# The gated convolution's shifted rows: TensorE products with shift matrices replaced by transfers inside SBUF and VectorE sums

## The reference

```
y_conv = c_b * conv(c_c * c_h, conv_w)        # causal, depthwise, width 3
conv(z)[s] = w[2] * z[s] + w[1] * z[s-1] + w[0] * z[s-2]     # z = 0 ahead of the first token
mix = concat([y_conv, y_gla]) @ w_out
```

## Time and profile before

| | |
|---|---|
| median of three runs | 2489.75 us (2489.63 to 2494.16) |
| profiled execution | 2493.07 us, its span 2491.3 us |
| TensorE matmul busy | 2393.9 us (96%) |
| VectorE busy | 1736.3 us (70%) |
| ScalarE busy | 1300.8 us (52%) |
| GpSimd busy | 100.2 us (4%) |
| DMA | 608.09 MB, mean 244 GB/s |
| mean granted TensorE clock | 0.988 of full |
| end of layer 0's mixer | about 110 to 184 us in the span |
| end of layer 1's mixer | about 455 to 510 us in the span |

### The profile page before, as it was taken

The page is one execution under the profiler, slowest core; times in us unless marked ns, Lnnn a source line. Parts: engine busy times, 40 slices in busy tenths (PEclk is TensorE's granted clock), DMA queues, the critical chain, the costliest instruction groups (busy, mean ns, idle before and its releaser), DMA issues.

```text
span 2491.3 us, 31286 instructions
## 1 busy us (share of the span) xinstructions
PE 2393.9 (96%) x11472; PEld 1927.8 (77%) x11472; DVE 1736.3 (70%) x1986; ACT 1300.8 (52%) x1661; POOL 100.2 (4%) x135
## 2 busy tenths in 40 slices
PE   7999989999999999999998999989999999999997
PEld 3668876768888888888886888878877887897885
DVE  2577775789999999999987446675467443556556
ACT  2334433458877777778873433444344433444442
POOL 1001001000000000000001000000000000000001
PEclk9999999999999999999998999999999999999998
DMA  9869857549999989989986563355536552336550
GB/s 365 302 212 331 321 203 240 182 166 391 393 323 363 393 307 374 380 318 383 362 307 204 175 211 126 118 183 202 202 125 221 181 207 91 125 116 235 202 186 34
DMA packets 316384, 608.09 MB, mean 244 GB/s; under 512 B 15106, under 2 KB 154402, under 8 KB 309603
## 3 DMA queue, kind: packets, MB, share of 16 engines
q1 hardware_dynamic: 306432, 564.27, 63.8%
q0 software_dynamic: 9552, 41.13, 4.5%
q10 hardware_dynamic: 274, 1.05, 0.1%
HBM read 605.31 MB, written 1.08 MB: 243 GB/s over the span
## 4 chain that ended last, share of the span: by engine, by line
PE 85%; DVE 7%; DMA 3%; ACT 2%; issue 1%; POOL 1%; DVEq 0%; ACTq 0%; SPq 0%
PE G L962 49%; PE A L962 29%; PE TB L962 4%; DMA down<-in_ada_w 2%; DVE w_lo L2947 1%; PE TB L1449 1%; POOL small L2755 1%; PE TB L984 1%; PE TB L1558 1%; DMA down<-in_moe_w_down 1%; DVE small L3385 1%; ACT probs L2177 0%; DVE x_tok L3397 0%; DVE u_lo L3291 0%; DVE small L2879 0%
## 5 line engine op out<-in xcount | busy, mean ns | idle before, releaser
L962 PE MATMUL G<-w_hi,u_hi 128*128 128x512 f32 x1592 | 622.2, 397 | 4.5 <-ACT u_hi L2519 2.1
L962 PE MATMUL G<-w_hi,u_lo 128*128 128x512 f32 x1592 | 612.1, 391 | 0.7 <-DVE u_lo L3291 0.7
L962 PE MATMUL G<-w_lo,u_hi 128*128 128x512 f32 x1592 | 612.3, 390 | 0.0
L2988 DVE TENSOR_TENSOR w_lo<-wide,w_hi 128x1024 fp32r<-128x1024 f32 x352 | 415.8, 1224 | 13.2 <-ACT w_hi L2245 3.8
L2245 ACT ACTIVATE w_hi<-wide 128x1024 fp32r<-128x1024 f32 x352 | 371.1, 1062 | 89.1 <-PE G L962 43.8
L962 PEld LDWEIGHTS G<-w_hi,u_hi 128*128 128x128 f32 x1592 | 298.9, 188 | 68.5 <-issue 4.1
L962 PEld LDWEIGHTS G<-w_hi,u_lo 128*128 128x128 f32 x1592 | 299.2, 188 | 65.9 <-DVE u_lo L3291 1.5
L962 PEld LDWEIGHTS G<-w_lo,u_hi 128*128 128x128 f32 x1592 | 299.9, 188 | 59.9
L962 PE MATMUL A<-w_hi,hidden_hi 128*128 128x512 f32 x772 | 301.6, 391 | 0.0
L962 PE MATMUL A<-w_hi,hidden_lo 128*128 128x512 f32 x772 | 300.8, 390 | 0.0
L962 PE MATMUL A<-w_lo,hidden_hi 128*128 128x512 f32 x772 | 300.6, 389 | 0.0
(11 more groups left out here) (447 smaller groups left out, 3177.7 us busy)
## 6 DMA issues: line engine op xcount, KB each, us to landing
down<-in_moe_w_down SPq DMA_DIRECT2D x176, 512.0 KB, 8.3
wide<-in_ffn_w_in SPq DMA_DIRECT2D x88, 1024.0 KB, 7.6
wide<-in_moe_w_gate SPq DMA_DIRECT2D x160, 512.0 KB, 8.2
wide<-in_moe_w_up SPq DMA_DIRECT2D x160, 512.0 KB, 8.9
down<-in_ffn_w_out SPq DMA_DIRECT2D x44, 1024.0 KB, 8.5
down<-in_ada_w SPq DMA_DIRECT2D x28, 1024.0 KB, 7.2
wide<-in_w_in SPq DMA_DIRECT2D x24, 1024.0 KB, 7.4
ada_row<-in_ada_w POOLq DMA_DIRECT2D x16, 1024.0 KB, 6.5
```

Of the source, the lines that this page charges most:

```text
L962: return nc.tensor.matmul(o, lhsT, rhs, start=start, stop=stop, skip_group_check=True)
L2988: V.tensor_tensor(w_lo[at % RING][:, :], raw_piece(n, at)[0], w_hi[at % RING][:, :].bitcast(F32), ALU.subtract).then_inc(lo_ready, 1)
```

## The change

TensorE's products with the shift matrices go, and so do the four matrices among the constants. ScalarE's queue copies z, rows moved down by one and by two partitions, from SBUF to SBUF: for each of the two shifts 112 rows of both tiles, then the rest of the rows, then the one or two rows that cross from tile 0 to tile 1. That is six transfers a layer, right behind ScalarE's piece 19. VectorE clears the first rows at p = 10, multiplies z itself by its weights at p = 18 (both tiles in one instruction of 128 x 1024), the two shifted copies at p = 22, and adds the three at p = 23. The rest of `between` stays, but the products at p = 22 stand ahead of the attention half's products with its gate, and the sums at p = 23 ahead of `out_rest`.

```diff
 # ScalarE
+                    def shift_rows():
+                        z, z2 = proj[:, :, C_C:C_C + CONV], proj[:, :, C_H:C_H + CONV]
+                        act.wait_ge(g_read, n.g + 8)
+                        for by, dst in ((1, z1), (2, z2)):
+                            act.dma_start(dst[by:by + EVEN], z[0:EVEN]).then_inc(conv_shifted, 16)
+                            act.dma_start(dst[by + EVEN:P], z[EVEN:P - by]).then_inc(conv_shifted, 16)
+                            act.dma_start(dst[0:by, 1, :], z[P - by:P, 0, :]).then_inc(conv_shifted, 16)
...
+                        if p == 19:
+                            shift_rows()
 # TensorE
-                        if p == 20:
-                            conv_sum(0)
-                        if p == 21:
-                            conv_sum(1)
 # VectorE
+                    def conv_rows():
+                        link(V.memset(z1[0:1, 0, :], 0.0))
+                        V.memset(proj[0:2, 0, C_H:C_H + CONV], 0.0).then_inc(conv_cleared, 1)
+
+                    def conv_term(back):
+                        z = (proj[:, :, C_C:C_C + CONV], z1, proj[:, :, C_H:C_H + CONV])[back]
+                        to = (proj[:, :, C_B:C_B + CONV], z1, proj[:, :, C_H:C_H + CONV])[back]
+                        if back == 0:
+                            dve.wait_ge(g_read, n.g + 8)
+                        else:
+                            dve.wait_ge(conv_cleared, arg + 1)
+                            dve.wait_ge(conv_shifted, 96 * (arg + 1))
+                        V.tensor_tensor(to, z, convw[:, WIDTH - 1 - back, :].unsqueeze(1).to_broadcast([P, T, CONV]),
+                                        ALU.mult).then_inc(conv_scaled, 1)
+
+                    def conv_add(back):
+                        dve.wait_ge(conv_scaled, 3 * arg + back + 1)
+                        if back == 2:
+                            dve.wait_ge(gla_conv_read, T * arg + 1)
+                        total = proj[:, :, C_B:C_B + CONV]
+                        V.tensor_tensor(total, total, (z1, proj[:, :, C_H:C_H + CONV])[back - 1], ALU.add) \
+                            .then_inc(gla_conv_read, 1)
...
                         if p == 10:
                             link(V.memset(state, 0.0))
+                            conv_rows()
                         if p == 18:
                             dve.wait_ge(s_gla, 32 * (arg + 1))
-                            conv_terms(0, 0)
-                            conv_terms(0, 1)
+                            conv_term(0)
                             mean_square(0)
                         if p == 19:
-                            conv_terms(0, 2)
                             mean_square(1)
                             normed(0)
                         if p == 20:
-                            conv_terms(1, 0)
-                            conv_terms(1, 1)
-                            conv_terms(1, 2)
                             normed(1)
+                        if p == 22:
+                            conv_term(1)
+                            conv_term(2)
-                        if p == 22:
-                            conv_read(0)
                         if p == 23:
-                            conv_read(1)
+                            conv_add(1)
+                            conv_add(2)
```

More of the change, by code:

```diff
@@ L37 @@
 WIDTH = 3
+EVEN = 112
 HEADS = 4
@@ L144 @@
 _col = 0
-for _name, _w in (("ident", P), ("shift1", P), ("shift2", P), ("cross1", P), ("cross2", P), ("cum", P),
+for _name, _w in (("ident", P), ("cum", P),
                   ("suffix", P), ("tri", P), ("ones", P), ("open", P), ("causal", P), ("slots", P), ("chunks", 2), ("experts", EXPERTS),
@@ L163, in constants @@
     put("ident", j == i)
[L164 to L167, removed]
     put("cum", same & (j <= i))
@@ L573, in build @@
         gla_y = sem("gla_half_ready")
-        gla_z = sem("conv_terms_ready")
-        gla_conv = sem("conv_sums")
-        gla_conv_read = sem("conv_sums_read")
+        conv_cleared = sem("conv_first_rows_cleared")
+        conv_shifted = sem("conv_rows_shifted")
+        conv_scaled = sem("conv_terms_scaled")
+        gla_conv_read = sem("conv_sums_ready")
         s_ln = sem("ln_params_loaded")
@@ L1939, in heads_out @@
                         last.then_inc(gla_out, 1)
[L1941 to L1950, removed]
                     def between(c, q):
@@ L3546, in normed @@
                         last.then_inc(gla_normed, 1)
[L3548 to L3555, removed]
-                        if which == 2:
-                            V.tensor_tensor(zc, zc, convw[:, 2, :], ALU.mult).then_inc(gla_z, 1)
-                    def conv_read(t):
-                        dve.wait_ge(gla_z, T * arg + t + 1)
-                        dve.wait_ge(gla_conv, T * arg + t + 1)
-                        V.tensor_tensor(proj[:, t, C_B:C_B + CONV], A[:, 1 - t, :], proj[:, t, C_C:C_C + CONV], ALU.add) \
+                    def conv_rows():
[17 more added lines that the diff above has]
+                        V.tensor_tensor(total, total, (z1, proj[:, :, C_H:C_H + CONV])[back - 1], ALU.add) \
                             .then_inc(gla_conv_read, 1)
@@ L3639, in read_out @@
                         if at == 0:
-                            dve.wait_ge(gla_conv_read, T * arg + b + 1)
+                            dve.wait_ge(gla_conv_read, T * arg + T)
                             return V.tensor_tensor(src[:, b, 0:CONV], gla_bank(c, b), dst, ALU.mult)
```

## The result

The change made the kernel slower. In 20 executions each, the kernel before had a median of 2492.99 us (2489.06 to 2495.68) and the changed one 2498.09 us (2493.77 to 2503.63). The ratio is worked out over all executions and not from the two medians, which lie 5.1 us apart: it is 1.0021, with a 95% interval from 1.0015 to 1.0027, so 5.2 us. That is clear of no change, and about as large as the 0.2% which the prediction took as the least that can be told. In a later series (10 executions beside 20 of before) it was 1.0017 (1.0008 to 1.0027). I had forecast +1.5 us and a range up to 2497, so the forecast was wrong: the sign was right, the size was not. "Slower" had 0.17 in the prediction, mostly for late transfers, which did not come.

What follows compares the result with a forecast made beforehand. TensorE carries 85% of the chain, but VectorE's queue was taken as the next limit. Constants -0.7, layer 0 -1.4, layer 1 +1.9 and clock +1.7 sum to +1.5: 2491.3 us, 8-in-10 range 2487 to 2497.

Steps and rivals of the forecast that it cites:

- Slower: Whole kernel: the chance, 0.17, of a time above 2494.7 us, the upper end of what can't be told from none.
- late transfers: Rival, both layers: VectorE's first shifted product waits for transfers landing late, +13.6 us, 2503.4 us; chance 0.12.
- the term for ScalarE's six issues in layer 1: ScalarE ahead of piece 20: issues take 3.0 us, only 1.72 free, so piece 22's high part comes 0.7 us later.
- layer 0's gain of 1.4: Layer 0, modulation rows' round trip: their sum comes at 147.0 instead of 148.45, the fold decides, 1.4 us gained.
- The transfers' traffic: Layer 0: loads for TensorE share the engines with the transfers; given as support for a late landing, without its own price.
- The forecast's gain of 2.1: Layer 0, output projection: TensorE starts at 146.2 instead of 148.31, gaining 2.1 us, not 5.2, and idling 3.0.
- VectorE's queue, layer 1: From piece 22, 8.1 us of VectorE work make `out_rest` and the output projection start 1.2 us later.
- The clock behind the projection's gap: Layer 1, output projection: after 5.6 us idle TensorE's clock is low for a while, 1.7 us lost.
- The constants: Start of the program: 256 of 845 KB fewer to load, 0.7 us gained, or 0 if something else binds.
- The transfers' landing: Both layers: transfers land in under 7 us, ahead of first need ten and 7.6 us on; costed at nothing.
- Full saving: Rival, both layers: TensorE's 10.3 us saving is paid in full as VectorE finishes sooner, 2478.7 us; chance 0.07.
- Clock stays up: Rival: TensorE's clock doesn't fall behind the new gaps, 2489.6 us; chance 0.22.

Runs made afterwards that it cites:

- second profile: A second profiled execution of the same changed kernel, nothing altered, read beside the first (2495.31 us): 2496.48 us.
- experiment 7: Changed kernel with the six issues spread on ScalarE's queue, two each behind pieces 18, 19 and 20: 2494.93 us, 1.0005 of the kernel before.
- experiment 4: Changed kernel without its transfers, their issues and the wait for them, so the convolution's rows stay unshifted: 2492.95 us, 1.0004 of the kernel before.
- experiment 8: Kernel before without TensorE's six shift products a layer and VectorE's wait for them, output wrong: 2488.53 us, 0.9983 of the kernel before.
- 1: Changed kernel with its six transfers a layer issued earlier, from GpSimd's queue instead of ScalarE's: 2494.39 us, 1.0008 of the kernel before.
- 2: Changed kernel with unread TensorE products filling the gap ahead of the output projection (two in layer 0, six in layer 1): 2497.65 us, 1.0018 of before.
- 6: Changed kernel with unread TensorE products in both gaps, ahead of piece 20 and of the output projection: 2496.38 us, 1.0016 of the kernel before.
- 11: Changed kernel with transfers from GpSimd's queue, shifted products at pieces 20 and 21, and unread products ahead of the output projection: 2490.83 us, 0.9987 of before.
- 3: Changed kernel with the four unused shift matrices back among the constants: 2501.68 us, 1.0032 of the kernel before, 7 executions.

## Why the prediction was wrong, step by step

Two terms of the sum failed.

**The first is the term for ScalarE's six issues in layer 1**: "six for 2.5 to 3.4, and I take 3.0", hence +0.7. I took 0.41 to 0.57 us each from issues at the start of the program; here they took 0.67 to 1.02 in layer 1 and 0.67 to 1.57 in layer 0. The high part of piece 20 came 2.5 us late and not 1.3, that of piece 22 (10.76 behind piece 19 in place of 8.79) 2.0 late and not 0.7. So layer 1 lost 26.15 - 24.19 = **2.0 us** by the issues, not 0.7, and 27.77 - 24.19 = **3.6** where the clock falls in the gap they make. The text did name the bound: over 0.6 us each, piece 22 would be late. Some luck is in this term: I let the issues begin at the end of piece 19, and they began with it, 1.06 us earlier. In layer 0 they cost TensorE nothing, as forecast, though they ended later than I had them.

**The second is layer 0's gain of 1.4**, where I had put the transfers at nothing and the round trip of the modulation rows at its old length. Measured are 1.1 us lost (76.93 against 75.79 from piece 17 to the feed-forward part) and 2.2 in the second profile.
- *The transfers' traffic.* That it would lengthen the loads of layer 0's modulation rows I had mentioned, among the rivals, and not priced. From VectorE's low part of piece 17 to the projection were 39.16 us before (109.15 to 148.31), 38.16 in the changed kernel, 38.97 in the second profile, 37.09 with the issues spread and 37.14 from GpSimd's queue. The forecast's gain of 2.1 is there without the collision (39.16 - 37.09 = 2.07); with it 1.0 and 0.2 are left. The **1.1 and 1.9 us** lost are the waits of 0.98 and 1.78 ahead of piece 20. The later waits fall into the idle time ahead of the projection, which is why that is 1.75 and not 3.0.
- *The round trip.* The modulation sum came 39.02 behind piece 17 in place of 39.30, so of 1.4 us 0.3 were gained; 1.35 in experiment 7. But the first transfer of the way out then took 5.16 us where it had taken 4.21 (chain in order of time, first the changed kernel, then before), and the fold came 50.93 behind piece 17 in place of 50.36.

```profile
148.06 5.16 DMA ada_kept<-ada_rows
```
```profile
149.44 4.21 DMA ada_kept<-ada_rows
```

It took 5.1 to 5.3 us in all the other runs where I read it, experiments 4 and 8 without any transfer of z too, so z's traffic isn't the reason. Which it is stays open. Even with no transfers layer 0 gains nothing (+0.2, experiment 4).
- *The clock.* It was at its lower level for part of 180 to 184 (0.59), behind a wait of 2.20 us; before, it had stayed at 1.00 behind one of 2.17.

**VectorE's queue, layer 1: right.** Forecast +1.2; with the issues out of the way (1, 4, 7) A is 1.24 to 1.25 longer than before, and the 8.1 us queue took 8.22.

**The clock behind the projection's gap: right.** Forecast 1.7 us behind a gap of 5.6; the gap was 5.40, and B shows 1.6 to 2.4 (16.41 to 17.19 against 14.8), all of it gone where the gap was filled (2, 6, 11). Together these two are the 2.9 us that I had forecast for layer 1 without the issues, and experiment 4 shows 3.0. What I didn't have is the second place where the clock can fall, ahead of piece 20.

**The constants: not settled.** Forecast -0.7; piece 17 stood 1.1 us earlier (109.15 to 108.07). But the same mark lies between 107.7 and 110.2 in the other profiles with the smaller constants, and between 109.1 and 110.7 in the three with the larger ones.

**The transfers' landing: right.** They were never waited for. On GpSimd's queue they landed after 6.7 to 8.6 us, so "under 7" was a little short.

**The sum.** Constants -1.1, layer 0 +1.1 and layer 1 +4.8 make +4.8 in the first profile, and -1.4 + 2.2 + 6.6 = +7.4 in the second; the ratio says +5.2. The two spans are only 2.2 and 3.4 longer. Of what is missing, 1.3 and 2.4 us are won between layer 0's feed-forward part and piece 19 of layer 1, where TensorE waits 1.2 us for a modulation row in the profile of before and 0 and 0.2 in these two; the rest is won behind layer 1's mixer, in part in the second block, where nothing was changed. That I can't explain; single executions of one kernel scatter by as much.

Of the 20 executions of the changed kernel the three longest (2501.68 to 2503.63) have a mean granted clock of 0.983 to 0.985, the three shortest 0.986 to 0.988. That falls of the clock make the long ones fits this and experiments 2 and 3. It isn't shown: in the second profile the clock fell in the gap too, and that execution took 2496.48, under the median.

**The rivals.** Full saving: dead (experiment 8: 4.2 us is all there is behind VectorE's queue as it was, even with nothing added to it). Late transfers: dead. Clock stays up: wrong behind the long gap.

## What to carry to other kernels

Price issues of transfers one by one on the queue of the engine that feeds the critical one, at what they cost there in the middle of work and not at the start, and put no more of them in one place than the idle time of that place holds. Ask too which loads are on their way at that moment and who waits for them: the same bytes, issued 2 to 7 us earlier, cost layer 0 nothing ahead of its projection. Taking work from the busiest engine pays only down to the next queue: before such a change, run the kernel without the work, as in experiment 8, and see what the prize is. A short gap on TensorE costs its own length, and sometimes nearly as much again through the clock (2.2 us and 1.6 here).

## What the runs showed of the hardware

- An issue on ScalarE's queue of a copy inside SBUF took 0.67 to 1.57 us in the changed kernel (up to 1.79 in the second profile), the 448 KB ones no longer than those of 2 or 4 KB (0.71 against 0.82 and 1.02 in layer 1). Behind its piece 19 ScalarE started nothing else until the last was issued.
- Behind a transfer that crawls on one DMA engine, the issue of the next one held the queue for 18.8 and 25.5 us, though it was for 2 KB, and ScalarE started nothing else: the issuing engine is stopped.
- The same gap (2.23 and 2.27 us) left the granted clock up in one execution and down for some 3 us in the next. It also fell behind waits of 1.95, 1.99 and 2.52 us, and stayed up behind one of 1.78.
- A copy inside SBUF, issued from GpSimd's queue, landed after 6.7 to 8.6 us (layer 0; 2 to 448 KB). In the changed kernel, with such copies on the way, loads of 1 MB took 7.8 to 11.5 us; without copies they took 4.9 to 8.0 (before and experiment 4), and with the copies begun 2.9 us earlier 5.6 to 8.5 (experiment 7).
